# A mixture-of-experts kernel on one core: down weights dealt to the partitions by pairs of neighbouring rows, share matrix turned by transposes

## What is computed

```python
gates = softmax(top_k(x @ w_router + b_router, 4))     # 32 experts, 4 for each token
gu    = xb @ w_gu[e] + b_gu[e]                         # w_gu[e]: 1024 x 2048, 8 MiB
gate  = minimum(gu[:, :1024], 7); up = clip(gu[:, 1024:], -7, 7)
hmid  = (up + 1) * gate * sigmoid(1.702 * gate)
y     = hmid @ w_down[e] + b_down[e]                   # w_down[e]: 1024 x 1024, 4 MiB
out[token] += y * gate_of_the_token                    # for the tokens that chose e
```

## Time and profile before

| what | us |
|---|---|
| median of three runs | 1316.4 |
| the profiled execution, whole | 1316.34 |
| its span, first to last instruction | 1314.3 |
| PE busy in the span (97%) | 1268.4 |
| DVE busy (36%) | 474.3 |
| ACT busy (15%) | 199.9 |
| gate and up products, L1012, busy | 464.6 |
| down products, L1038, busy | 245.7 |
| combine products, L985, busy | 105.3 |
| bytes moved by DMA | 450.56 MB, mean 343 GB/s |

### The profile page before, as it was taken

One profiled execution on the slowest core, in us unless ns is written; L12 is line 12 of the kernel. 1 busy time (PEld: TensorE's weight loads), 2 busy tenths in 40 slices (PEclk: granted clock), 3 DMA queues, 4 the chain that ended last, 5 costly groups with the idle time before them and its releaser, 6 DMA issues.

```text
span 1314.3 us, 19250 instructions
## 1 busy us (share of the span) xinstructions
PE 1268.4 (97%) x7201; PEld 554.5 (42%) x7201; DVE 474.3 (36%) x990; ACT 199.9 (15%) x347; POOL 65.7 (5%) x146
## 2 busy tenths in 40 slices
PE   7999989989899999999999999999999999999996
PEld 5887757665433333333333333333333333333321
DVE  1183775355453322223333222233232222222344
ACT  3123522223410000000000000000000000000002
POOL 3002102001400000000000000000000000000000
PEclk9999999999899999999999999999999999999998
DMA  9343308329599999999999999999999999999994
GB/s 300 134 164 133 99 4 257 144 73 373 231 362 405 417 417 417 417 418 418 418 418 418 418 418 417 417 417 417 419 418 418 418 418 418 418 417 417 417 417 176
DMA packets 104068, 450.56 MB, mean 343 GB/s; under 512 B 11746, under 2 KB 21080, under 8 KB 71160
## 3 DMA queue, kind: packets, MB, share of 16 engines
q1 hardware_dynamic: 98964, 446.18, 84.8%
q10 hardware_dynamic: 5068, 3.89, 1.1%
HBM read 443.88 MB, written 6.26 MB: 342 GB/s over the span
## 4 chain that ended last, share of the span: by engine, by line
PE 46%; DMA 21%; SPq 3%; DVE 1%; issue 0%; ACT 0%
PE ps L1012 23%; DMA ring<-in_w_gu 19%; PE ps L1038 11%; PE ps L985 5%; PE ps L964 4%; SPq L371 2%; DMA ring<-in_w_down 2%; PE ps L978 1%; SPq L376 1%; PE ps L972 1%; PE ps L993 1%; PE ps L1002 1%; PE ps L1031 0%; DVE x_tok L1827 0%; DVE x_tok L1769 0%
## 5 line engine op out<-in xcount | busy, mean ns | idle before, releaser
L1012 PE MATMUL ps<-ring,proj 128*64 128x512 f32 x2024 | 464.6, 598 | 7.0 <-DMA ring<-in_w_gu 7.0
L1038 PE MATMUL ps<-ring,proj 128*64 128x512 f32 x1024 | 245.7, 602 | 2.3 <-DMA ring<-in_w_down 1.8
L1012 PEld LDWEIGHTS ps<-ring,proj 128*64 128x64 f32 x2024 | 137.0, 137 | 253.9 <-issue 201.6
L1744 DVE TENSOR_SCALAR proj<-ps 128x512 f32<-128x512 f32 x32 | 22.1, 691 | 395.8 <-PE ps L1012 394.8
L1769 DVE TENSOR_TENSOR x_tok<-x_tok,ps 96x512 f32<-96x512 f32 x192 | 122.7, 679 | 98.9 <-PE ps L985 98.9
L1038 PEld LDWEIGHTS ps<-ring,proj 128*64 128x64 f32 x1024 | 64.7, 136 | 153.7 <-issue 146.3
L985 PE MATMUL ps<-proj 64*96 64x512 f32 x384 | 105.3, 627 | 0.6 <-DVE proj L1758 0.6
L615 PE MATMUL ps<-feat,ring 128*128 128x280 f32 x384 | 97.0, 404 | 0.0
L583 PE MATMUL ps<-feat,ring 128*128 128x280 f32 x384 | 92.9, 405 | 0.2 <-DVEq L1352 0.2
L583 PEld LDWEIGHTS ps<-feat,ring 128*128 128x128 f32 x384 | 73.8, 193 | 18.8 <-DVE feat L1351 0.5
L615 PEld LDWEIGHTS ps<-feat,ring 128*128 128x128 f32 x384 | 71.2, 191 | 19.6 <-issue 3.3
(11 more groups left out here) (361 smaller groups left out, 887.0 us busy)
## 6 DMA issues: line engine op xcount, KB each, us to landing
ring<-in_w_gu SPq DMA_DIRECT2D x253, 1024.0 KB, 19.3
ring<-in_w_down SPq DMA_DIRECT2D x128, 1024.0 KB, 22.1
ring<-in_w_in SPq DMA_DIRECT2D x11, 2048.0 KB, 8.9
ring<-in_w_in SPq DMA_DIRECT2D x2, 1024.0 KB, 8.4
out<-states SPq DMA_DIRECT2D x1, 2048.0 KB, 8.7
ring<-in_w_oa SPq DMA_DIRECT2D x1, 2048.0 KB, 9.1
ring<-in_w_ob SPq DMA_DIRECT2D x1, 2048.0 KB, 11.8
ring<-in_w_out SPq DMA_DIRECT2D x1, 2048.0 KB, 8.0
```

What stands on the lines that cost most here:

```text
L1012: last = mm(bank(j // 2)[64 * (j % 2):64 * (j % 2) + 64, :], xgT[:, k % 4, k // 4, :], w[:, 512 * j:512 * j + 512], start=False, stop=k == ...
L1038: last = mm(bank(4)[64 * j:64 * j + 64, :], hidT[:, k % 4, 64 * (k // 4):64 * (k // 4) + 64], ring[:, KT + k // 2, n:n + 512], start=False ...
L1744: ts(hid_g, bank(0), SWIGLU_LIMIT, None, ALU.min).then_inc(sg["gate_clipped"], 1)
```

## The change

Two parts. The down weights: partition p of a down load gets rows 2p and 2p + 1 of the 256, which lie next to one another, 8 KB in one run. So the hidden values have to be turned in the same order: of the four transposes in `turn_hid`, two take the even and the odd columns of the first 256 columns of `hid`, and two those of the second 256 (a column step of 2 floats). The products of `down` stay as they are. The share matrix: `turn_share` uses transposes (`tr`) in place of products with the identity; shapes and places stay.

```diff
@@ down_load
                 sp.dma_start(ring[:, KT + k, :].rearrange("p (j n) -> p j n", j=2),
-                             src.rearrange("(j p) n -> p j n", p=128)).then_inc(w_arrived[KT + k], 16)
+                             src.rearrange("(p j) n -> p j n", p=128)).then_inc(w_arrived[KT + k], 16)
@@ turn_share
                 for i in range(NI):
-                    last = mm(bank(7)[:, TP * i:TP * i + TP], hotg[:, i, :], ident[0:TP, 0:TP], start=True, stop=True)
+                    last = tr(bank(7)[:, TP * i:TP * i + TP], hotg[:, i, :], ident[0:TP, 0:TP])
                 last.then_inc(sg["share_turned"], 1)
@@ turn_hid
                 for c in range(4):
-                    last = tr(hid_T[:, c, :], hid[:, 128 * c:128 * c + 128], ident[:])
+                    last = tr(hid_T[:, c, :], hid[:, 256 * (c // 2) + c % 2:256 * (c // 2) + 256:2], ident[:])
                 last.then_inc(sg["hid_turned"], 1)
```

## The result

The changed kernel takes 1305.6 us in the median of four runs (1304.76 to 1306.43), the kernel before 1316.29 us beside it; the ratio is 0.9917 with a 95% interval of 0.9900 to 0.9934. That is 10.7 us less. The profiled execution of the changed kernel took 1306.43 us, its span is 1304.7 us against 1314.3.

What follows compares the result with a forecast made beforehand. The prediction took DMA to bound the loop, with TensorE close behind. From 1316.34 us it took 10.2 for down loads and 0.84 for `turn_share` in the tail, giving 1305.3 us, range 1303.0 to 1311.5 us.

Steps and rivals of the forecast that it cites:

- What bounds the kernel: In the expert loop DMA binds at 30.12 us a block; TensorE needs 29.20 us and has 10.95 us of room.
- Down loads, 10.2 us: 120 down loads of experts 1 to 30 go from 408 to 422 GB/s, 10.2 us less.
- The 0.085 us a load: Saving for each 1 MiB down load in the loop, from 2.570 to 2.485 us.
- sum of the two levels, 30.16 us: One block's loads in the loop: 4.194 MB at 408 and 8.389 MB at 422 GB/s, 10.28 + 19.88 us.
- window of down loads alone: Window before the loop in which the four down loads were said to flow alone, at 408 GB/s.
- The choice of 422 between the bounds of 408 and 422: Rate taken for down loads in 8 KB runs, as gate and up loads show in length, order and destination.
- The rival that took the 416 GB/s of other loads with 4 KB rows for the price of the down loads: Only part of the down loads' gap comes from run length: 4.3 us gained, 1311.2 us; chance 0.14.
- an estimated 4.7 us: Smaller gain over the 120 down loads by the skill page's packet and descriptor costs, giving 1310.8 us in all.
- `turn_share`, 0.84 us: Transposes save 0.42 us for each turning; hidden by DMA in the loop, 0.84 us in the tail.
- `turn_hid`, 0: The four transposes of the hidden values, read with a step of two floats, cost nothing more.
- the upper end: In `turn_hid`, stepped loads take twice as long: 0.56 us more a block, 3.1 us worse in all.
- The sum: Whole kernel: 1316.34 us less 10.2 for down loads and 0.84 for the tail, 1305.3 us.

Runs made afterwards that it cites:

- the kernel with less TensorE work alone: The kernel before with the share matrix turned by transposes, down weights as before: 1314.96 us, ratio 0.9993.
- the runs of 4 KB in the new order: The changed kernel with each down load cut in two of 512 KB, rows 2p, then rows 2p + 1: 1315.68 us, ratio 0.9998.
- in the old one without jumps: The kernel before with share transposes and each down load cut in two, rows p, then rows 128 + p: 1315.27 us, ratio 0.9996.
- The kernel with the rows part alone: The changed kernel with the share matrix turned by identity products again, down weights still dealt anew: 1308.32 us, ratio 0.9938.

## Why the prediction was right, point by point

*What bounds the kernel.* Right. The loop follows the DMA rate: from 418 to 422 GB/s a round became 30.12 - 29.83 = 0.29 us shorter, and the kernel with less TensorE work alone was only 1.1 us faster.

*Down loads, 10.2 us.* Right in mechanism and nearly in size. From the first L1038 x12 of the chain to the end of the last wait it is 1276.46 - 426.74 = 849.72 us now and was 1285.34 - 426.28 = 859.06 us, 9.3 us less. Counted from the start of the span the wait ends 1285.34 - 1276.46 = 8.9 us sooner, which is 30 rounds by 0.29 us. The 0.085 us a load was a little high: a round fell by 0.29 us, not 0.34. The prediction's own sum of the two levels, 30.16 us, lay above the 30.12 us of the chain, and the 29.82 us that 422 GB/s give is what came. Its window of down loads alone was also not that: 13 us at 408 GB/s are 5.3 MB, and four down loads are 4.19; the level stands by the stretches of 10 us in the loop. The choice of 422 between the bounds of 408 and 422 was the right one, and its reason is now shown and not only argued: the runs of 4 KB in the new order, and in the old one without jumps, both stayed at 408 or 409. The rival that took the 416 GB/s of other loads with 4 KB rows for the price of the down loads falls with these two runs. The packets in that window of 4 us took 160.5 ns, 3 ns less than the 4 KB packets of the down loads; why is not shown.

*The price of a packet.* Measured with runs of 4, 8 and 16 KB, 408, 422 and 429 GB/s are 160.6, 310.6 and 611 ns for one of 16 engines, about 150 ns for each 4 KB and 10 to 11 ns for each packet. The single packets, whose records overlap a little, give 12 to 13 ns. The rule of the Trainium skill, "DMA: Bandwidth & Descriptors", section "Why small descriptors are slow (HBM only)", about 3 cycles for each packet, had made an estimated 4.7 us of the change. At the 850 MHz that the same page of the Trainium skill gives the fabric in its section "Specifications", 10.6 ns are by estimate 9 cycles. So the rule has the direction, and the price here is about three times as high; the measurement decides.

*`turn_share`, 0.84 us.* Right: 0.44 and 0.43 us in the tail, nothing in the loop. The kernel with the rows part alone has the same loop to 0.02 us.

*`turn_hid`, 0.* Wrong by a little. A load with step 2 takes 209 ns, not 141:

```profile
L993 PEld LDWEIGHTS ps<-ident,proj x128: 194/209/219, 383.1 to 1278.9; 128*128 128x128 f32 x128
```

That is half way to the upper end. Much of it lies beside the products: the chain has 0.52 us instead of 0.46 in the tail, and a block in the loop is 28.85 us where 28.78 was the sum. DMA covers it here. The run with the rows part alone shows how thin the cover would have been without the transposes: blocks of 29.29 us, TensorE in the chain until 1205 us, and the loop's end just not later.

*The tail.* 1314.3 - 1285.34 = 28.96 us before, 1304.7 - 1276.46 = 28.24 us after: 0.72 us. That is the 0.87 of the two turnings less 0.06 for the stepped loads; the other 0.1 us lies behind the second turning.

*The sum.* 9.3 + 0.72 is 10.0 us; the loop began 0.5 us later in the profiled execution after, and the spans differ by 9.6. The medians differ by 10.7 us against 11.0 forecast (1316.34 - 1305.3). Agreement to 0.3 us is luck: by the traces the terms came about 1 us too high, and the four runs lie 1.7 us apart.

## What to carry to other kernels

When a rate stands flat for most of the span, split it by which transfers flow in each stretch: two levels, with the cheaper form already in the kernel, give the price of a change before it is made. Lengthen runs by dealing neighbouring rows to one partition and pay with the order of the other operand. But count what a bigger load does at the end, where nothing is left to hide the wait for it, and what every small load added for the new order does at the start.

## What the runs showed of the hardware

A packet cost an engine some 10 ns beside its bytes even at 4 and 8 KB: 408, 422 and 425 to 430 GB/s with runs of 4, 8 and 16 KB; at 4 KB neither the order of the rows nor a load of 512 KB instead of 1 MiB changed it. A 128 x 128 float32 load of the array took 141 ns with step 1 and 209 ns with step 2, and also 209 ns with step 4:

```profile
L993 PEld LDWEIGHTS ps<-ident,proj 128*128 128x128 f32 x128 | 17.8, 209 | 25.2 <-issue 25.2
```

(the run with down weights of 16 KB; line, engine, operation, tiles and count, busy us and mean ns). The Trainium skill, "SBUF — State Buffer", section "Door 1: The DMA port swizzle (why `[64,N]` ≈ `[32,N]`)", lets a step of up to four such values pass without loss. These loads do not agree with it, and the measurement decides: step 2 costs 68 ns on top of 141, and step 4 no more than step 2.

With 1024 pieces of 4 bytes more in the parameter loads TensorE's first instruction waited for 29.5 us instead of 7.6.
